# Attention of a two-layer decoder trunk: low parts of all weight panels on VectorE, and another order of scores, value sums and the late weight split

## The chip, the core and the metric

The kernel runs on one core of a Trainium2 chip. The metric is the device time of one execution in microseconds (us); lower is better. The core has a matrix engine (TensorE; PE in the profile, with its weight loads as PEld), three engines for elementwise work (VectorE or DVE, ScalarE or ACT, GpSimd or POOL) and queues that start transfers (those of SyncE, SP, and of GpSimd here). Each engine works through its own list of instructions in order, and the lists meet only at semaphores.

## The reference, cut to what matters

The input is one sequence of 512 tokens with 1024 features, in float32. Layer 0 has sixteen attention heads of 64 features: eight with a dilated window and a linear bias, eight with a forgetting bias. Layer 1 is a retention layer. Each is followed by a squared-ReLU MLP with 4096 hidden features, and a last norm closes the trunk. The change touches the attention of layer 0 alone.

```python
def _rms_norm(x, g):
    y = xf * lax.rsqrt(jnp.mean(xf * xf, axis=-1, keepdims=True) + RMS_EPS)
    return (y * g).astype(x.dtype)

def _dilated_branch(q, k, v, slopes, window, dilation):        # 8 heads
    logits = scores * dh**-0.5 - slopes * dist, masked to the dilated causal window
    # softmax inside each of the three dilations, then a softmax over their log-denominators

def _forgetting_attention(q, k, v, log_f):                     # 8 heads
    sc = q k^T * dh**-0.5 + c_i - c_j   (c = cumsum(log f)), causal
    return softmax(sc) @ v

def _even_mixer(h, w_in, b_f, w_out, slopes):
    proj = h @ w_in                    # q, k, v of both kinds of head, and the forget gates
    ...
    o = jnp.concatenate([_merge_heads(oa), _merge_heads(ob)], axis=-1)
    return o @ w_out

def reference(x, ...):
    for layer in range(2):
        h = _rms_norm(x, norm_mix_g[layer])
        x = x + (_even_mixer(h, ...) if layer % 2 == 0 else _odd_mixer(h, ...))
        h = _rms_norm(x, norm_ffn_g[layer])
        x = x + jnp.square(jax.nn.relu(h @ w1)) @ w2
    return _rms_norm(x, final_g)
```

## The kernel before

**Numbers in two parts.** Large products are not done in one float32 pass. An operand is kept as a high part (ScalarE rounds it with a copy) and a low part (the rest, by a subtraction), and three products are added: high by high, high by low, low by high. So each weight block of 128x128 costs three matmuls, and each weight panel has to be split before use: `split` on ScalarE (line 1460) writes the high part of a quarter of a panel, and a subtraction writes the low part. The subtraction is on VectorE (`split`, line 2107) for most panels, and on GpSimd (`split_lo`, line 3066) for panels 5 and 6 (`POOL_PANELS`).

**Panels and jobs.** Layer 0's projections use eight weight panels (`E_PANELS`: values, queries and keys by pairs of heads, and the two halves of the output weight). A panel has four quarters and serves four jobs; a job is eight k-tiles of three matmuls each with 512 columns, into one PSUM bank. Jobs 0 to 24 are the input projections (job 4 the gates, job 24, `LAST_KEY`, the last keys), jobs 25 to 32 the output projection, of which 25 to 28 use panel 6 and 29 to 32 panel 7.

**Attention beside the jobs.** `STEPS` and `TAIL` say which attention work stands beside which job. A step (h, g, v, pair) does four things: the scores of head h, the splitting of head g's probabilities into a high and a low f16 part, the value product of head v, and the transposition of a finished pair of heads. On PE, `beside` divides a step into ten points n = 0 to 9 that are spread between the k-tiles, and `attention` says what stands at which point: `gather_values(v)` (20 small matmuls, into `pv`), the three `scores_unit(h, u)` (u = 0 has 512 columns, u = 1 has 384, u = 2 has 256 and 128), and `turn_output(pair)`.

**What each head passes through.** PE scores; DVE `logits` (adds the bias table and takes the row maximum, line 2293); ACT `exps`; ACT `parts_hi` and DVE `parts_lo` (line 2302); the SP queue turns the parts by a DMA transposition into `turned_main`, one buffer for all heads but 13 and 15, which have their own; PE `gather_values`; DVE `value_sum` (a reduction, line 2314); GpSimd `normalise`; PE `turn_output`; ACT `output_hi` and DVE `output_lo` (line 2329) give the operand `oT` of the output projection. For heads 8 to 15 GpSimd adds the causal mask to the bias table just before each logits instruction (`mask`, line 3072), and the mask of the smallest query blocks waits until the logits of unit 1 are done.

**What sets the order.** Every engine's order is written out by hand. Scores use two banks in turn, so `scores_unit(h, 0)` waits for the first logits of head h - 1's unit 2. ACT copies a finished job to `q_stack` or `k_stack` (lines 1848 and 1852) only after that step's `exps`, and DVE takes the low part of it (lines 2388, 2392, and 2337 for job 24) before the next head's logits. The SP queue takes weight quarters and transpositions in one order; a quarter is fetched once `lo_split` says that the quarter before it in the same buffer is split. The k-tiles 6 and 7 of jobs 25 to 28 stand at the end (`EARLY_KT = 6`), after the last pair is transposed.

## Time and profile before

| | us |
|---|---|
| median of 3 runs (1263.57 to 1263.76) | 1263.6 |
| the profiled execution | 1263.39 |
| its span, first to last instruction | 1261.6 |
| PE busy (99% of the span) | 1243.1 |
| DVE busy (74%) | 932.4 |
| ACT busy (61%) | 767.5 |
| POOL busy (24%) | 296.6 |

The profiled execution lies 0.2 us from the median, and 1.8 us of it lie outside the span. Busy time is what an engine's instructions cover. A busy PE need not be at its best: its clock can be granted at half speed, and a matmul's duration holds its pipeline, so that the next one starts before it ends. The idle time of an engine that nobody waits for costs nothing.

### The profile page before, as it was taken

Reading aid. Unit: us, or ns where it says so; the run is one execution under the profiler, and the core shown is the slowest. Engines: PE = TensorE matmul, PEld = TensorE weight load, DVE = VectorE, ACT = ScalarE, POOL = GpSimd, SP = SyncE. Lnnn points to the kernel's source line nnn. Section 1 sums busy time; section 2 is a strip of 40 time slices with the busy share of each in tenths; the row PEclk is TensorE's granted clock in tenths of the full one; section 3 lists DMA queues with packets and bytes.
Section 4 is the critical chain, followed back from the end, with each engine's and each line's share of the span. In section 5 each row is a group of like instructions: output and inputs, shape, how many; then the busy total and the mean of one; then the engine's idle time right before and its main releaser. Section 6 shows DMA issues by size and latency. Waiting matters only on the chain.

```text
span 1261.6 us, 19374 instructions
## 1 busy us (share of the span) xinstructions
PE 1243.1 (99%) x7446; PEld 1096.2 (87%) x7446; DVE 932.4 (74%) x1196; ACT 767.5 (61%) x1064; POOL 296.6 (24%) x330
## 2 busy tenths in 40 slices
PE   9999998999999999999999999999999999999997
PEld 6788777798898988989898889898889899898996
DVE  6577646588759587598756797567899967859678
ACT  6677754477465474666646655556667757457474
POOL 2443653112111121111142212231231122111220
PEclk9999999999999999999999999999999999999999
DMA  7366456769998989983968597968589899898993
GB/s 249 91 142 153 120 150 130 242 139 229 229 236 209 226 170 235 233 234 93 214 132 184 155 244 165 225 145 221 110 220 242 199 212 228 215 235 198 207 217 101
DMA packets 147979, 238.95 MB, mean 189 GB/s; under 512 B 51104, under 2 KB 72872, under 8 KB 147888
## 3 DMA queue, kind: packets, MB, share of 16 engines
q0 software_dynamic: 32352, 102.79, 43.3%
q1 hardware_dynamic: 115232, 134.60, 34.0%
q8 instruction: 59, 0.97, 0.3%
q10 hardware_dynamic: 304, 0.33, 0.1%
q14 instruction: 32, 0.26, 0.1%
HBM read 127.57 MB, written 2.11 MB: 103 GB/s over the span
## 4 chain that ended last, share of the span: by engine, by line
PE 90%; DVE 4%; ACT 3%; issue 2%; DMA 1%; POOL 0%; SPq 0%; POOLq 0%; DVEq 0%; ACTq 0%
PE bank L945 22%; PE bank L977 18%; PE bank L1352 11%; PE bank L1420 6%; PE pv L977 5%; PE bank L1302 5%; PE bank L1143 4%; PE pv L945 4%; PE bank L1083 3%; PE bank L1244 2%; PE bank L1110 2%; PE bank L1316 1%; PE bank L1366 1%; PE pv L1366 1%; ACT arena L1781 1%
## 5 line engine op out<-in xcount | busy, mean ns | idle before, releaser
L2221 DVE TENSOR_TENSOR w<-raw_tiles,w 128x1024 fp32r<-128x1024 f32 x312 | 371.2, 1221 | 90.4 <-ACT w L1562 90.2
L1562 ACT ACTIVATE w<-raw_tiles 128x1024 fp32r<-128x1024 f32 x312 | 315.4, 1051 | 122.7 <-PE bank L977 56.2
L3159 POOL DMA_DIRECT2D raw_tiles<-raw_tiles x176 | 152.3, 908 | 629.5 <-DVE w L2221 360.0
L945 PE MATMUL bank<-h_ops,w 128*128 128x256 f32 x2304 | 281.4, 283 | 0.0
L945 PEld LDWEIGHTS bank<-h_ops,w 128*128 128x128 f32 x2304 | 278.9, 192 | 0.7
L977 PE MATMUL bank<-w,arena_q 128*128 128x512 f32 x1044 | 241.3, 389 | 0.0
L977 PEld LDWEIGHTS bank<-w,arena_q 128*128 128x128 f32 x1044 | 195.3, 188 | 40.1
L1352 PE MATMUL bank<-w,h_ops 128*128 128x512 f32 x624 | 143.9, 390 | 0.0
L1352 PEld LDWEIGHTS bank<-w,h_ops 128*128 128x128 f32 x624 | 116.6, 188 | 23.8
L1143 PE MATMUL bank<-hT_hi,w 128*128 128x512 f32 x224 | 78.2, 398 | 0.0
L1644 ACT ACTIVATE arena_q<-arena 128x1024 fp32r<-128x1024 f32 x40 | 42.5, 1062 | 47.0 <-PE pv L977 19.8
L1420 PE MATMUL bank<-w,arena_q 128*128 128x512 f32 x288 | 68.6, 393 | 0.0
L977 PE MATMUL pv<-w,arena_q 128*128 128x512 f32 x288 | 67.9, 389 | 0.0
L977 PEld LDWEIGHTS pv<-w,arena_q 128*128 128x128 f32 x288 | 54.1, 188 | 11.2
L1420 PEld LDWEIGHTS bank<-w,arena_q 128*128 128x128 f32 x288 | 53.3, 188 | 10.9 <-DVE x L2823 0.2
L2493 DVE TENSOR_TENSOR arena_q<-arena,arena_q 128x1024 fp32r<-128x1024 f32 x40 | 48.8, 1221 | 18.4 <-ACT arena_q L1644 17.8
L1302 PEld LDWEIGHTS bank<-h_ops,w 128*128 128x128 f32 x504 | 60.9, 192 | 0.2
L1302 PE MATMUL bank<-h_ops,w 128*128 128x256 f32 x504 | 60.9, 283 | 0.0
L1781 ACT ACTIVATE arena<-arena,negmax 128x512 f32<-128x512 f32 (+1 forms) x64 | 35.6, 558 | 34.2 <-DVE negmax L2293 34.2
L2471 DVE TENSOR_TENSOR arena<-arena,bank 128x512 f32<-128x512 f32 x48 | 32.7, 684 | 29.7 <-PE bank L945 29.7
L1143 PEld LDWEIGHTS bank<-hT_hi,w 128*128 128x128 f32 x224 | 42.1, 188 | 8.2
L945 PE MATMUL pv<-h_ops,w 128*128 128x256 f32 x384 | 48.7, 283 | 0.0
(268 smaller groups left out, 1817.8 us busy)
## 6 DMA issues: line engine op xcount, KB each, us to landing
raw_tiles<-raw_tiles POOLq DMA_DIRECT2D x176, 512.0 KB, 5.5
raw_tiles<-in_ffn_w_in SPq DMA_DIRECT2D x64, 512.0 KB, 5.8
raw_tiles<-in_ffn_w_out SPq DMA_DIRECT2D x64, 512.0 KB, 6.7
raw_tiles<-in_odd_w_in SPq DMA_DIRECT2D x32, 512.0 KB, 5.5
raw_tiles<-in_even_w_in SPq DMA_DIRECT2D x48, 256.0 KB, 3.3
raw_tiles<-in_odd_w_in SPq DMA_DIRECT2D x32, 256.0 KB, 5.3
raw_tiles<-in_odd_w_out SPq DMA_DIRECT2D x16, 512.0 KB, 6.0
raw_tiles<-raw_tiles POOLq DMA_DIRECT2D x20, 256.0 KB, 4.2
```

The lines of the kernel that those rows point to most:

```text
L945: mm = pe.matmul(bank[first + b][:, 256 * m:256 * m + 256], w_slots[use_slot(use)][:, p, k, c:c + P], h_ops[:, H_BLOCK[op], q, k, :], star ...
L977: mm = pe.matmul(bank[first + t][:, :], a_ring[a_slot(g, i)][:, a, k, P * t:P * t + P], w_slots[use_slot(use)][:, b, k, :], start=(starts ...
L1143: mm = pe.matmul(bank[e_bank(j)][:, :], stat(k, a), mov(k, b), start=(k == 0 and i == 0), stop=(k == KT - 1 and i == 2))
L1302: mm = pe.matmul(dst, w_slots[use_slot(use)][:, p, k, c:c + P], h_ops[:, H_BLOCK[op], q, k, :], start=(starts and k == 0 and n == 0), stop ...
L1352: mm = pe.matmul(bank[first + b][:, :], h_ops[:, H_BLOCK[op], p, k, P * b:P * b + P], w_slots[use_slot(use)][:, q, k, :], start=(i < 3 and ...
L1420: mm = pe.matmul(bank[first + t][:, :], operand[:, k, P * t:P * t + P], w_slots[use_slot(use)][:, b, k, :], start=(starts and m == 0), sto ...
L1562: nc.scalar.activation(w_flat(use_slot(use), 0, half), raws[tile][:, 1024 * half:1024 * half + 1024], ACT.Copy).then_inc(m_hi, 1)
L1644: nc.scalar.activation(a_ring[a_slot(g, i)][:, 0], a_source(1, op), ACT.Copy).then_inc(a_hi, 1)
L1781: nc.scalar.activation(v, v, ACT.Exp, bias=negmax[:, h % 2, c:c + 1], scale=-1.0, accum_out=den[:, pair % 2, k:k + 1]).then_inc(prob_ready, 1)
L2221: nc.vector.tensor_tensor(w_flat(use_slot(use), 1, half), raws[use_tile(key)][:, 1024 * half:1024 * half + 1024], w_flat(use_slot(use), 0, ...
L2493: nc.vector.tensor_tensor(slot[:, 1], a_source(1, SECOND[i][0]), slot[:, 0].bitcast(F32), ALU.subtract).then_inc(a_lo, 1)
L3159: pool.dma_start(raws[dst][:, part], raws[src][:, part], accum_op=ALU.add).then_inc(t_made[value][half], 16)
```

## The change

The change leaves the arithmetic alone. It moves eight subtractions from GpSimd to VectorE and writes several orders anew:

- The low parts of panels 5 and 6 (eight quarters) are taken by DVE: seven of them at the head of jobs 17 to 23, the eighth (quarter 3 of panel 6) after the first step of the tail. The high part of that eighth one moves on ACT from the end of job 24 to the same place of the tail.
- On PE the value product stands at point 2 in place of point 1 of the steps that have scores, except heads 12 and 15 (point 1) and 14 (point 0). The scores of heads 13, 14 and 15 move to later points.
- On DVE `value_sum` stands between the logits of units 1 and 2 (before: ahead of unit 1), and for heads 14 and 15 `value_sum` comes ahead of `parts_lo`, which is spread over the step.
- The k-tiles of jobs 25 to 28 stand in another order, with k-tile 6 of all four ahead of the last k-tile 7, which alone waits for the last pair.

```diff
@@ -331,7 +331,6 @@
 
 UNIT_BLOCKS = (4, 3, 3)
 UNIT_AT = (0, 8 * P, 14 * P)
-POOL_PANELS = range(5, 7)
 TURNS = ((0,), (1, 2))
 TURN_OF = {u: d for d, units in enumerate(TURNS) for u in units}
 
@@ -1182,9 +1181,9 @@
             def attention(h, g, v, pair, n):
 
 
-                if n == (0 if h == 14 else 1) and v is not None:
+                if n == {12: 1, 14: 0, 15: 1}.get(h, 2 if h is not None else 1) and v is not None:
                     gather_values(v)
-                at = (4, 6, 8) if h == 12 else (0, 3, 6)
+                at = {12: (4, 6, 8), 13: (1, 4, 7), 14: (4, 6, 8), 15: (2, 4, 6)}.get(h, (0, 3, 6))
                 if n in at and h is not None:
                     scores_unit(h, at.index(n))
                 if n == 5 and pair is not None:
@@ -1203,14 +1202,14 @@
                 beside(STEPS.get(j - 1, []), [(j, k) for k in range(KT)])
 
             last = STEPS[24]
-            beside(last[0:1], [(25, 0), (25, 1), (25, 2), (25, 3)])
-            beside(last[1:2], [(25, 4), (26, 0), (26, 1), (26, 2), (26, 3)])
-            beside(TAIL[0:1], [(26, 4), (25, 5), (26, 5), (27, 0), (27, 1), (27, 2)])
-            beside(TAIL[1:2], [(27, 3), (27, 4), (27, 5), (28, 0), (28, 1), (28, 2)])
-            beside(TAIL[2:3], [(28, 3), (28, 4)])
-            beside(TAIL[3:4], [(28, 5)])
+            beside(last[0:1], [(25, 0), (25, 1), (25, 2), (25, 3), (26, 0)])
+            beside(last[1:2], [(25, 4), (26, 1), (26, 2), (26, 3), (26, 4)])
+            beside(TAIL[0:1], [(27, 0), (27, 1), (27, 2), (25, 5), (26, 5)])
+            beside(TAIL[1:2], [(27, 3), (27, 4), (27, 5), (28, 0), (28, 1)])
+            beside(TAIL[2:3], [(28, 2), (28, 3), (28, 4)])
+            beside(TAIL[3:4], [(28, 5), (25, 6), (26, 6), (27, 6), (28, 6)])
             for j in range(25, 29):
-                out_part(j, range(EARLY_KT, KT))
+                out_part(j, [KT - 1])
             for j in range(29, 33):
                 e_job_free(j)
                 out_part(j, range(KT))
@@ -1855,8 +1854,6 @@
                         last.then_inc(aev, 1)
                     for st in STEPS.get(j, []):
                         step(*st, j + 1 if early_split(j + 1) else None)
-                    if j == LAST_KEY:
-                        split_for(j)
                 if n == 0:
 
                     act.wait_ge(job_done, GATE_JOB + 1)
@@ -1869,6 +1866,8 @@
                 if n == 5:
                     for st in TAIL:
                         step(*st)
+                        if st[1] == NHEAD - 1:
+                            split_for(LAST_KEY)
 
 
             norm_tiles(1)
@@ -2339,19 +2338,29 @@
                 done.then_inc(lev, 1)
 
             def step(h, g, v, pair):
-                if h is not None:
+                if h in (14, 15):
                     logits(h, 0)
-                if h == 14:
-                    dve.wait_ge(aev, e_aev(LAST_KEY))
-                    key_lo(LAST_KEY, 1)
-                if g is not None:
-                    for u in range(3):
-                        parts_lo(g, u)
-                if v is not None:
+                    if h == 14:
+                        dve.wait_ge(aev, e_aev(LAST_KEY))
+                        key_lo(LAST_KEY, 1)
                     value_sum(v)
-                if h is not None:
                     logits(h, 1)
+                    parts_lo(g, 0)
                     logits(h, 2)
+                    parts_lo(g, 1)
+                    parts_lo(g, 2)
+                else:
+                    if h is not None:
+                        logits(h, 0)
+                    if g is not None:
+                        for u in range(3):
+                            parts_lo(g, u)
+                    if h is not None:
+                        logits(h, 1)
+                    if v is not None:
+                        value_sum(v)
+                    if h is not None:
+                        logits(h, 2)
                 if pair is not None:
                     output_lo(pair)
 
@@ -2375,7 +2384,7 @@
                         for st in STEPS[j]:
                             step(*st)
                         continue
-                    if kind != "out" and n + 1 not in POOL_PANELS:
+                    if kind != "out" and j != LAST_KEY:
                         split(n + 1, q, n % 2)
                     if kind == "v":
                         value_rest_of(j)
@@ -2397,8 +2406,6 @@
                             dve.wait_ge(x_landed[q], 32)
                         residual(out_bank(j), i, q, j + 1)
                         if n < 7:
-                            if q == 0:
-                                dve.wait_ge(lo_split, 4 * 7)
                             split(n + 1, q, n % 2)
                         elif q < 2:
                             w_lo(0, 0, q)
@@ -2415,6 +2422,8 @@
                 if n == 5:
                     for st in TAIL:
                         step(*st)
+                        if st[1] == NHEAD - 1:
+                            split(6, 3, 1)
                 if n == 0:
 
                     dve.wait_ge(gate_low, 1)
@@ -3059,13 +3068,6 @@
                 nc.gpsimd.tensor_tensor(table[:, h % 2, :], table[:, h % 2, :], lncount,
                                         ALU.add).then_inc(table_ready, 1)
 
-            def split_lo(n, c):
-
-                pool.wait_ge(hi_split, 4 * n + c + 1)
-                pool.wait_ge(lo_split, 4 * n + c)
-                nc.gpsimd.tensor_tensor(panel_quarter((n + 1) % 2, 1, c), raw[:, c],
-                                        panel_quarter((n + 1) % 2, 0, c).bitcast(F32), ALU.subtract).then_inc(lo_split, 1)
-
             def mask(h, tb, dst=None):
 
                 own = table[:, h % 2, P * tb:P * tb + P]
@@ -3117,27 +3119,20 @@
             first_masks(9)
             bias_table(10)
             later_masks(9)
-            split_lo(5, 0)
             normalise(3)
             first_masks(10)
             bias_table(11)
             later_masks(10)
-            split_lo(5, 1)
             value_third(4)
             first_masks(11)
             bias_table(12)
             later_masks(11)
-            split_lo(5, 2)
             value_third(5)
             bias_table(13)
             first_masks(12)
-            split_lo(5, 3)
             value_third(6)
-            split_lo(6, 0)
             value_third(7)
-            split_lo(6, 1)
             later_masks(12)
-            split_lo(6, 2)
             first_masks(13)
             bias_table(14)
             normalise(4)
@@ -3148,7 +3143,6 @@
             normalise(5)
             first_masks(15)
             later_masks(15)
-            split_lo(6, 3)
             normalise(6)
             pool.wait_ge(score_done, 3 * NHEAD)
             load_gain(1)
```

Three places as the programs have them. First, VectorE beside job 24, in the step of head 13 (value product of head 10): `parts_f` is head 12's probabilities, `o_odd` the output of the value sum, and the rows with a bank are logits. Before:

```order
L2302 SCALAR_TENSOR_TENSOR parts_f<-arena,parts_f 128x512
L2302 SCALAR_TENSOR_TENSOR parts_f<-arena,parts_f 128x384 x2
L2314 TENSOR_REDUCE o_odd<-pv 128x4x64
L2319 RECIPROCAL rden<-den 128x8
L2293 ISA arena,negmax<-bank,arena 128x384
L2293 ISA negmax 128x1
L2293 ISA arena,negmax<-bank,arena 128x256
```

and now:

```order
L2301 SCALAR_TENSOR_TENSOR parts_f<-arena,parts_f 128x512
L2301 SCALAR_TENSOR_TENSOR parts_f<-arena,parts_f 128x384 x2
L2292 ISA arena,negmax<-bank,arena 128x384
L2292 ISA negmax 128x1
L2313 TENSOR_REDUCE o_odd<-pv 128x4x64
L2318 RECIPROCAL rden<-den 128x8
L2292 ISA arena,negmax<-bank,arena 128x256
```

The reduction and the reciprocal have moved behind the logits of 384 columns, ahead of those of 256 and 128.

Second, TensorE beside jobs 25 and 26, in the step of head 14, right behind the value product of head 11: rows with `arena_q` are scores, rows x3 with `arena_r` are k-tiles of the output projection. Before:

```order
L1040 MATMUL bank<-arena_q 128x512
L1042 MATMUL bank<-gain_q,arena_q 128x512
L1083 MATMUL bank<-w,arena_r 128x512 x3
L1040 MATMUL bank<-arena_q 128x384
L1042 MATMUL bank<-gain_q,arena_q 128x384
L1083 MATMUL bank<-w,arena_r 128x512 x3
L1040 MATMUL bank<-arena_q 128x256
L1042 MATMUL bank<-gain_q,arena_q 128x256
L1040 MATMUL bank<-arena_q 128x128
L1042 MATMUL bank<-gain_q,arena_q 128x128
L1083 MATMUL bank<-w,arena_r 128x512 x3
```

and now:

```order
L1082 MATMUL bank<-w,arena_r 128x512 x6
L1039 MATMUL bank<-arena_q 128x512
L1041 MATMUL bank<-gain_q,arena_q 128x512
L1082 MATMUL bank<-w,arena_r 128x512 x3
L1039 MATMUL bank<-arena_q 128x384
L1041 MATMUL bank<-gain_q,arena_q 128x384
L1082 MATMUL bank<-w,arena_r 128x512 x3
L1039 MATMUL bank<-arena_q 128x256
L1041 MATMUL bank<-gain_q,arena_q 128x256
L1039 MATMUL bank<-arena_q 128x128
L1041 MATMUL bank<-gain_q,arena_q 128x128
L1082 MATMUL bank<-w_raw,arena_r 128x512 x3
```

Two k-tiles now stand ahead of the first scores of head 14 (before: none), the third and the fourth, which opens job 26, stand ahead of the second and the third scores, and the k-tile of `w_raw` follows the scores.

Third, VectorE in the same step: `gain_q` is the low part of the last keys, a head at a time, and `parts_own_60` head 13's probabilities. Before:

```order
L2337 TENSOR_TENSOR gain_q<-bank,arena_q 64x512
L2293 ISA arena,negmax<-bank,arena 128x512
L2293 ISA negmax 128x1
L2337 TENSOR_TENSOR gain_q<-bank,arena_q 64x512
L2302 SCALAR_TENSOR_TENSOR parts_own_60<-arena,parts_own_60 128x512
L2302 SCALAR_TENSOR_TENSOR parts_own_60<-arena,parts_own_60 128x384 x2
L2314 TENSOR_REDUCE o_odd<-pv 128x4x64
L2293 ISA arena,negmax<-bank,arena 128x384
```

and now:

```order
L2336 TENSOR_TENSOR gain_q<-bank,arena_q 64x512
L2292 ISA arena,negmax<-bank,arena 128x512
L2292 ISA negmax 128x1
L2336 TENSOR_TENSOR gain_q<-bank,arena_q 64x512
L2313 TENSOR_REDUCE o_odd<-pv 128x4x64
L2292 ISA arena,negmax<-bank,arena 128x384
L2292 ISA negmax 128x1
L2301 SCALAR_TENSOR_TENSOR parts_own_60<-arena,parts_own_60 128x512
L2292 ISA arena,negmax<-bank,arena 128x256
```

The value sum and the logits of unit 1 have moved ahead of the splitting of head 13's probabilities, of which one part now stands between two logits.

## Rows read from the trace of the kernel before

**Rows 1.** PE's waits, 60 to 300 us: who for whom, us, times, longest.
```profile
PE bank L1040 <- DVE negmax L2293: 4.2, 3, 2.3
PE pv L1059 <- DMA turned_main<-parts_r: 1.8, 3, 1.0
PE bank L1040 <- DVE gain_q L2337: 1.4, 1, 1.4
PE bank L1083 <- DVE arena_r L2329: 0.7, 1, 0.7
PE bank L1070 <- DVE o_odd L2324: 0.4, 1, 0.4
PE pv L1059 <- issue: 0.4, 1, 0.4
```
**Rows 2.** Windows: length, each engine's busy time, granted clock, DMA share, GB/s.
```profile
201.00:206.00 5.00, 5.00 (x31) 4.38 (x30) 4.04 (x9) 2.57 (x10) 1.56 (x3) 0.66 0.41 77
255.00:600.00 345.00, 345.00 (x2271) 317.89 (x2270) 271.07 (x282) 216.40 (x250) 58.62 (x73) 1.00 0.83 203
```
**Rows 3.** PE in order of time: start, duration, instruction, idle before it.
```profile
65.34 0.39 PE L1143 MATMUL bank<-hT_lo,w_raw 128*128 128x512 f32 x1
...
66.03 0.39 PE L1143 MATMUL bank<-hT_lo,w_raw 128*128 128x512 f32 x1
...
72.23 0.26 PE L1059 MATMUL pv<-v_parts,turned_main 128*128 128x192 bf16 x1 [1.01 <-DMA turned_main<-parts_r]
...
193.97 0.47 PE L1040 MATMUL bank<-arena_q 128*128 128x512 f32 x1 [1.36 <-DVE gain_q L2337]
...
200.55 0.50 PE L1040 MATMUL bank<-arena_q 128*128 128x512 f32 x1 [2.30 <-DVE negmax L2293]
```
**Rows 4.** PEld in order of time, job 25 behind the scores of head 15.
```profile
209.04 0.53 PEld L1083 LDWEIGHTS bank<-w_raw,arena_r 128*128 128x128 f32 x3 [0.42 <-DVE arena_r L2329]
```
**Rows 5.** DVE in order of time, step of head 9.
```profile
137.56 0.94 DVE L2314 TENSOR_REDUCE o_odd<-pv 128x256 f32<-128x768 f32 x1
...
139.68 0.42 DVE L2293 CUSTOM_DVE_ANT_0 arena<-bank,arena 128x256 f32<-128x256 f32 x1 [0.71 <-POOL arena L3072]
```
**Rows 6.** POOL in order of time, at panel 6.
```profile
163.02 2.40 POOL L3066 TENSOR_TENSOR w<-raw_tiles,w 128x1024 fp32r<-128x1024 f32 x1
165.39 1.16 POOL L3045 TENSOR_TENSOR v_parts<-v_rest_f,v_parts 128x512 bf16<-128x512 f32 x1
```
**Rows 7.** DVE in order of time, at jobs 17 and 23.
```profile
141.79 0.69 DVE L2365 TENSOR_TENSOR v_rest_f<-bank,v_parts 128x512 f32<-128x512 f32 x1 [1.47 <-ACT v_parts L1838]
...
184.46 1.39 DVE L2388 SCALAR_TENSOR_TENSOR arena_q<-bank,arena_q 64x512 fp32r<-64x512 f32 x2 [2.06 <-ACT arena_q L1848]
```
**Rows 8.** Order of time around job 24: ACT.
```profile
191.93 2.40 ACT L1852 ACTIVATE arena_q<-bank 64x512 fp32r<-64x512 f32 x4
```
**Rows 9.** DVE in order of time, behind job 24.
```profile
193.14 0.68 DVE L2337 TENSOR_TENSOR gain_q<-bank,arena_q 64x512 fp32r<-64x512 f32 x1 [1.25 <-ACT arena_q L1852]
194.81 0.69 DVE L2293 CUSTOM_DVE_ANT_0 arena<-bank,arena 128x512 f32<-128x512 f32 x1 [0.98 <-PE bank L1042]
```
**Rows 10.** The buffer of the turned parts: time from issue to landing of its DMAs.
```profile
DMA to landing us min/median/max: 3.2/3.8/5.0
```
**Rows 11.** POOL and DVE in order of time, last quarter of panel 6.
```profile
210.22 2.38 POOL L3066 TENSOR_TENSOR w_raw<-raw_tiles,w_raw 128x1024 fp32r<-128x1024 f32 x1 [3.72 <-ACT w_raw L1460]
```
**Rows 12.** DVE in order of time, the same stretch, one instruction.
```profile
210.69 2.46 DVE L2302 SCALAR_TENSOR_TENSOR parts_own<-arena,parts_own 128x512 f16<-128x512 f32 x1 [1.71 <-ACT parts_own L1793]
```
**Rows 13.** DVE, 60 to 227 us: forms, count, busy us, mean ns, idle before.
```profile
L2107 DVE TENSOR_TENSOR w<-raw_tiles,w 128x1024 fp32r<-128x1024 f32 x6 | 7.5, 1254 | 0.0
L2302 DVE SCALAR_TENSOR_TENSOR parts_r<-arena,parts_r 128x512 f16<-128x512 f32 x10 | 6.9, 686 | 0.0
```
**Rows 14.** DVE in order of time, residuals of jobs 25 and 26.
```profile
227.35 0.69 DVE L2214 TENSOR_TENSOR x<-bank,x 128x512 f32<-128x512 f32 x1 [1.12 <-PE bank L1083]
...
229.09 0.69 DVE L2214 TENSOR_TENSOR x<-bank,x 128x512 f32<-128x512 f32 x1
```

## The prediction, made before the changed kernel had run

> **What bounds the kernel now.** I read the windows first, then PE's waits, then the order of time on each engine around every wait. From 255 to 600 us PE is busy in all 345.00 of 345 us at full clock [rows 2], and later stretches read the same: behind the attention the kernel is PE's own work, and whatever the attention saves or costs moves the end by as much. So the question is how much PE loses between 60 and 230 us. Its waits there are ten stops with 8.9 us together (4.2 + 1.8 + 1.4 + 0.7 + 0.4 + 0.4) [rows 1]. A stop costs more than its idle time: a matmul of 512 columns is drawn 0.39 us long, but three start within 0.69 us (65.34 to 66.03), one each 0.23 [rows 3], so idle time is counted from an end 0.16 us after the next start was due. Ten times 0.16 is 1.6. Behind the longest stop (2.30 us at 200.55, 1.36 us at 193.97 just ahead of it) [rows 3] the granted clock is 0.66 on average over 201 to 206 us [rows 2]: part of these 5 us ran at 1.2 in place of 2.4 GHz, and 5 x 0.34 = 1.7 us of work are lost. One wait is hidden in the weight loads, 0.42 us for the operand of pair 5 [rows 4]; PE covers some of it and I count 0.3. In all 8.9 + 1.6 + 1.7 + 0.3 = 12.5 us could be won, no more.
>
> **Value products a point later.** Three stops (1.8 us, the first 1.01) wait for the turned parts of a head [rows 1, 3]; the other two share 0.8. The transposition is released by `parts_lo`, whose place on DVE is the same, and the product now stands one k-tile, 0.69 us, later. Of the first stop 0.3 stays, the others go: 1.5, with two drains 1.8 us. Bounds: nothing (if the landing moves along) to 2.3.
>
> **The chain from logits to logits.** Two stops of 1.9 us together (4.2 less the 2.30) are first scores, of heads 10 and 13, that wait for the last logits of the head before [rows 1]. In the masked steps DVE does the value sum (0.94), then unit 1, and then idles 0.71 until GpSimd has masked for unit 2 [rows 5]; eight such waits exist. With the value sum between the two that idle time is covered: each masked step is 0.7 shorter on DVE, and ACT's exponentials of unit 1 run beside the value sum. Ahead of head 10 two such steps follow each other, 1.4 against a stop of 0.99; head 13 gets 0.7 and a k-tile of 0.69 more on PE against 0.9. Both go: 1.9 with two drains 2.2. Bounds: 0.7 (the shorter chain alone, once) and 2.2.
>
> **Eight subtractions from GpSimd to DVE.** GpSimd needs 2.40 for one, and `value_third` starts only behind it: 163.02 + 2.40, then 1.16 to 166.5 [rows 6], where the value product of head 8 stops for 0.4 with "issue" as releaser [rows 1]. That stop goes: 0.6 with its drain. On DVE a split takes 1.25 [rows 13]. At jobs 17 to 23 DVE idles seven times ahead of the row that the split now precedes, least at the first (1.47) and 2.06 at the last [rows 7]; the eighth place, in the tail, has more than 2 us too. The cover is ACT's copy of a finished job or GpSimd's third value part, and each idle time is longer than the split, so I take zero; without cover each costs 1.25, all eight 10.
>
> **Heads 14 and 15.** The copy of the last keys runs on ACT from 191.93 [rows 8], behind head 13's exponentials; its low part is done at 193.14 + 0.68 = 193.8 [rows 9], and head 14's first scores start at 193.97 after 1.36 idle [rows 3]. Two masked steps (12 and 13) now end 0.7 earlier each, so these scores may start near 192.5. PE arrives, by its own work, at 193.97 - 1.36 = 192.6, less 1.06 for the stop of head 13, plus 2 x 0.69 for the two k-tiles put ahead: 192.9. No stop is left. Call that start s. DVE's answer begins 0.84 later (194.81 against 193.97) [rows 3, 9]; logits and the second low part of the keys end at s + 2.25, value sum at 3.1, unit 1 at 3.65, the first third of `parts_lo` (0.69) [rows 13] at 4.35, unit 2 at 4.8. PE asks for that at the first scores of head 15: scores, three k-tiles, a value product of 1.4 and a last k-tile put them at s + 6.2. So the 2.30 goes too, and with it the reason of the low clock: 1.36 + 2.30 + 1.7 + two drains = 5.7, and the hidden 0.3. Bounds: 0.7 to 6.0. New is a wait inside: k-tile 0 of job 26 needs the bank of job 24, hence the second low part of the keys at s + 2.25, and PE is there after scores, k-tile and scores (0.46 + 0.69 + 0.35) at s + 1.5: **0.8 us lost**, 0 to 1.5. Behind that stop nothing but PE queues; DVE does not wait for it. Also new: value products 10, 11 and 12 stand closer together (heads 13, 14 and 15 use three different points), and each transposition into the one buffer starts when the product before has read it. A landing takes 3.8 us, 5.0 at most [rows 10]; against some 5.5 us between products the margin is used up by the issue of two DMAs. I take **0.5** of 0 to 2.4.
>
> **The tail.** Two stops, 0.4 and 0.7 [rows 1], wait for the last pair. Now k-tiles 6 of jobs 25 and 26 stand ahead of its transposition (1.4 us against 0.4 + 0.16) and two k-tiles behind it, 1.4, where one k-tile and the stop made 0.69 + 0.16 + 0.72 = 1.6: **0.2 stays**. Won: 1.4 in all. But jobs 25 to 28 now end 0.69 apart, not 1.38, and behind each DVE adds the residual and splits a quarter of panel 7: 1.74 us a pair (227.35 to 229.09) [rows 14]. The fourth quarter is ready some 0.2 + 4 x 1.74 = 7.2 us after job 25; PE asks for it at 3 x 0.69 + 3 x 1.38 = 6.2. **1.1 lost** with a drain, 0 to 1.5; before, it was asked for at 8.3 and cost nothing.
>
> **Sum.** Won: 1.8 + 2.2 + 0.6 + 5.7 + 0.3 + 1.4 = 12.0. New or left inside: 0.8 + 0.5 + 0.2 + 1.1 = 2.6. From the profiled execution, 1263.4: 1263.4 - 9.4 = **1254.0**. That execution lies 0.2 under the median, so the median reads the same within it.
>
> **A rule against the change.** A split reads two operands in SBUF while GpSimd masks read theirs. The trace shows such a pair once: GpSimd's subtraction runs from 210.22 to 212.60 [rows 11], and DVE's first third of `parts_own`, started at 210.69, takes 2.46 in place of 0.69 [rows 12, 13], that is until 0.55 after GpSimd's end. The Trainium skill (SBUF — State Buffer, "SBUF: two separate sides") calls the port that these two engines share an exclusive lock that is held for the whole instruction; by that rule the trace agrees. It cuts both ways: the 1.8 us at 210 go with GpSimd's subtractions (DVE has them to spare there), and each new DVE split can hold a mask up for 1.25.
>
> **Rivals.** (1) The late order stays bound by another engine: heads 14 and 15 still wait for DVE, ACT or the mask, at other places, and the clock still falls. For it: DVE has five kinds of work within 6 us there; against it: the slack of 1.4 found above. 5.7 of the win is gone, part of the new waits too: 1263.4 - 4.2 = 1259.2. (2) The landings follow the products, since one buffer serves them: 1.8 is not won and 0.3 more is lost at heads 11 and 12: 1256.1. For it: one buffer; against it: the stops came with an early release by the product and a late one by `parts_lo`. (3) Splits block masks: three of the eight stand just ahead of a masked head (jobs 17, 18, 23), 1.25 each on the logits' chain: 1257.8. Against it: at jobs 17 to 22 PE has whole jobs without scores to catch up. (4) The other side: DVE becomes the bound. If the idle times at jobs 17 to 23 are used up, because ACT and PE arrive earlier as well, the eight splits lie on the chain to PE, 8 x 1.25 = 10.0, and two waits long enough to bring the clock down add 2 x 1.7: 1254.0 + 13.4 = 1267.4. It decides once the splits cost over 9.4, that is nearly all of them; the shortest idle time, 1.47, is over a split. (5) The new orders never meet the waits: same time as before, 1263.4.
>
> **Chances.** Forecast 0.62, rival 1 0.15, rival 2 0.11, rival 3 0.06, rival 4 0.03, rival 5 0.03. The range: best case 1263.4 - 12.5 = 1250.9 needs every bound at its good end; I start at 1251.5, and take in rivals 1, 2 and 3 up to 1260.0. A measurement here tells 0.2%, 2.5 us, from no change. Faster than 1261.1: 0.92; within: 0.05; slower: 0.03.
>
> **What would show it.** Right: PE's waits between 60 and 230 us sum to 2 to 3.5 us; none over 1.2; the granted clock is 1.00 in every window there; no 0.71 of DVE for a mask in steps with a value sum; DVE's splits at jobs 17 to 23 with hardly a change of PE; short waits for `w` at k-tiles 2, 4 and 6 of job 29. Wrong: a stop over 1.5 us near the last keys, a second one at each value product, or a window at half clock.

## The result, and the profile after

The changed kernel takes 1254.41 us (median of 4 runs, 1254.35 to 1255.75) against 1263.61 for the kernel before (1263.57 to 1263.76): a ratio of 0.993 with an interval of [0.9912, 0.9947]. The forecast was 1254.0. The profiled execution took 1254.46 with a span of 1252.3, 9.3 less than the span before. Line numbers of PE, DVE and ACT in the kernel after are one smaller than before: L1058 and L1060 are the value product, L1039 and L1041 the scores, L1082 the k-tiles, L2292 the logits, L2313 the value sum, L2106 a split.

PE's waits of the kernel after, 60 to 300 us (waiting line and releaser: us in total, times, longest), answer to [rows 1]:

```profile
PE pv L1058 <- DMA turned_main<-parts_r: 1.3, 2, 0.8
PE bank L1082 <- DVE gain_q L2336: 0.6, 1, 0.6
```

Ten stops with 8.9 us have become three with 1.9 (2 to 3.5 were forecast). The windows of the kernel after (busy time of PE, PEld, DVE, ACT, POOL with instructions, then the granted clock, DMA share and GB/s) answer to [rows 2]:

```profile
60.00:230.00 170.00, 167.93 (x999) 138.80 (x998) 126.28 (x263) 117.04 (x255) 61.22 (x65) 1.00 0.64 156
201.00:206.00 5.00, 5.00 (x40) 4.21 (x38) 4.61 (x8) 2.65 (x6) 1.37 (x1) 1.00 0.90 169
255.00:600.00 345.00, 344.98 (x2238) 316.40 (x2237) 271.93 (x286) 213.78 (x248) 60.77 (x73) 1.00 0.84 205
```

The same stretch of the kernel before, in the same view:

```profile
60.00:230.00 170.00, 161.01 (x957) 132.16 (x956) 110.97 (x248) 112.64 (x251) 74.89 (x72) 0.99 0.60 143
```

PE is busy 6.9 us more in the 170, and the clock no longer falls. DVE has 15 us more to do there and GpSimd 14 less: the subtractions moved, and the stretch now reaches some 9 us further into the program. Behind 255 us PE is as busy as it was, so the lead is carried to the end undiminished: the same instruction (the first transposition of the second norm) starts at 242.08 before and 232.69 after, 9.4 earlier.

What is left sits in three places. First PE, by the order of time; one row for each stop:

```profile
72.19 0.26 PE L1058 MATMUL pv<-v_parts,turned_main 128*128 128x192 bf16 x1 [0.55 <-DMA turned_main<-parts_r]
...
187.31 0.26 PE L1058 MATMUL pv<-v_parts,turned_main 128*128 128x192 bf16 x1 [0.77 <-DMA turned_main<-parts_r]
...
191.84 0.96 PE L1082 MATMUL bank<-w,arena_r 128*128 128x512 f32 x3 [0.58 <-DVE gain_q L2336]
```

The first is the stop of head 2, once 1.01 and now a k-tile later; the second is new, in the value product of head 11: the transposition that it waits for is issued at 180.58, right behind the last matmul of head 10's product (180.28), which now stands a k-tile later; the third is k-tile 0 of job 26 behind the second low part of the keys. Then weight loads (PEld of the kernel after, with the idle time ahead of each row), which answer to [rows 4]. The first row is the last k-tile of jobs 25 to 28, which waits for the operand of the last pair; the others belong to job 29:

```profile
217.59 2.61 PEld L1082 LDWEIGHTS bank<-w_raw,arena_r 128*128 128x128 f32 x12 [0.45 <-DVE arena_r L2328]
220.60 1.22 PEld L1082 LDWEIGHTS bank<-w,arena_r 128*128 128x128 f32 x6 [0.40 <-issue]
222.27 1.23 PEld L1082 LDWEIGHTS bank<-w,arena_r 128*128 128x128 f32 x6 [0.45 <-DVE w L2106]
224.00 1.23 PEld L1082 LDWEIGHTS bank<-w,arena_r 128*128 128x128 f32 x6 [0.51 <-DVE w L2106]
```

A third wait for `w`, of 0.51 too, follows at 225.73. The three fall every 1.73 us, which is DVE's pace (the kernel after, DVE):

```profile
220.40 0.68 DVE L2213 TENSOR_TENSOR x<-bank,x 128x512 f32<-128x512 f32 x1
221.00 1.21 DVE L2106 TENSOR_TENSOR w<-raw_tiles,w 128x1024 fp32r<-128x1024 f32 x1
222.13 0.68 DVE L2213 TENSOR_TENSOR x<-bank,x 128x512 f32<-128x512 f32 x1
222.73 1.21 DVE L2106 TENSOR_TENSOR w<-raw_tiles,w 128x1024 fp32r<-128x1024 f32 x1
```

Residual and split take DVE 1.73 a pair, as in [rows 14], and PE's two k-tiles take 1.38: job 29 walks behind DVE. Last, a masked step of DVE in the kernel after (head 12), against [rows 5]:

```profile
175.57 0.54 DVE L2292 CUSTOM_DVE_ANT_0 arena<-bank,arena 128x384 f32<-128x384 f32 x1
176.05 0.07 DVE L2292 DVE_READ_ACCUMULATOR2_ANT negmax<- 128x1 f32 x1
176.05 0.94 DVE L2313 TENSOR_REDUCE arena<-pv 128x256 f32<-128x768 f32 x1
176.92 0.41 DVE L2292 CUSTOM_DVE_ANT_0 arena<-bank,arena 128x256 f32<-128x256 f32 x1
```

The value sum stands between unit 1 and unit 2, and no idle time stands ahead of unit 2: the 0.71 is gone.

### The profile page after: what moved, and what is told of

It reads as the page before. It is cut to its first block, busy times and chain, and to the rows that moved or that the text cites. A ratio compares the mean times of both kernels' runs of the same rounds, so it can differ in the third digit from the quotient of the medians.

```text
span 1252.3 us, 19365 instructions
## 1 busy us (share of the span) xinstructions
PE 1240.8 (99%) x7446; PEld 1095.0 (87%) x7446; DVE 940.9 (75%) x1204; ACT 768.4 (61%) x1064; POOL 282.5 (23%) x322
## 4 chain that ended last, share of the span: by engine, by line
PE 95%; DVE 2%; DMA 1%; issue 1%; ACT 1%; SPq 0%; POOLq 0%; POOL 0%; DVEq 0%; ACTq 0%
PE bank L944 22%; PE bank L976 18%; PE bank L1351 11%; PE bank L1142 7%; PE bank L1419 6%; PE pv L976 5%; PE bank L1301 5%; PE pv L944 4%; PE bank L1082 3%; PE bank L1243 2%; PE bank L1109 2%; PE bank L1315 1%; PE bank L1365 1%; PE pv L1365 1%; PE pv L1058 1%; PE pv L1351 1%
```

## The experiments

All times are compared with runs of the kernel before on the same chip. Three groups of runs gave medians of 1263.42, 1263.67 and 1262.67 for it. These differ since its executions fall into two groups, around 1262.0 and around 1263.6; under `fill_stops` stands what the runs show of the reason. The intervals belong to the ratios. Differences under 1 us between medians of such mixed executions say little.

**splits_only**: the kernel before with the eight subtractions on DVE.

```diff
-                    if kind != "out" and n + 1 not in POOL_PANELS:
+                    if kind != "out" and j != LAST_KEY:
                         split(n + 1, q, n % 2)
...
-            split_lo(5, 0)
...
```

> The kernel before with the eight subtractions of panels 5 and 6 on VectorE, every order else as before. Theory of the prediction (each split stands in idle time of VectorE): the stop of 0.4 us before head 8's value product goes, about 0.6 us faster, 1263.0; the clock still falls near 202 us. Rival (VectorE is the bound, the splits lie on its chain): up to 8 x 1.25 = 10 us slower, and the first scores of heads 10 to 14 wait longer for logits. Rival (the shared port: splits hold up masks): 1 to 4 us slower.

1262.96 us, ratio 0.9994 [0.9984, 1.0003]. The stop of head 8's value product with releaser "issue" is gone, and no other has grown by as much (a new one of 0.27 stands at head 11's product): PE's stops sum to 8.3. So the 10 us of new DVE work are free, as forecast, and what they win is too small for the ratio to tell from nothing. Taken group by group, which the interval does not cover, it may be the forecast 0.6: the three lowest of the ten runs lie at 1261.4 to 1261.6, the five lowest of the 20 of the kernel before at 1261.9 to 1262.3.

**value_sum_only**: the kernel before with the value sum between units 1 and 2, except at heads 14 and 15.

```diff
-                if v is not None:
+                if h in (14, 15):
                     value_sum(v)
-                if h is not None:
                     logits(h, 1)
                     logits(h, 2)
+                else:
+                    if h is not None:
+                        logits(h, 1)
+                    if v is not None:
+                        value_sum(v)
+                    if h is not None:
+                        logits(h, 2)
```

> The kernel before with one move on VectorE: the value sum stands between the logits of units 1 and 2 for all heads but 14 and 15. Theory: each masked step is 0.7 us shorter on VectorE, so the stops before the first scores of heads 10 and 13 (0.99 and 0.90 us) go, and head 14's first scores (1.36) wait some 1.4 less: 2.2 to 4.5 us faster, 1259.1 to 1261.4. Rival (the chain is bound by ACT's copies of finished jobs, not by VectorE): under 1 us.

1258.08 us, ratio 0.9963 [0.9949, 0.9977]. PE's waits of this kernel:

```profile
PE bank L1040 <- DVE negmax L2293: 2.3, 1, 2.3
PE pv L1059 <- DMA turned_main<-parts_r: 1.0, 1, 1.0
PE bank L1083 <- DVE arena_r L2329: 0.7, 1, 0.7
PE bank L1070 <- DVE o_odd L2324: 0.4, 1, 0.4
PE bank L1040 <- DVE gain_q L2337: 0.3, 1, 0.3
```

This is the largest single part, 4.7 by the ratio (the interval allows 2.9 to 6.4), more than the theory had even at its best (1259.1). The spans of two profiled executions in both of which the clock fell, 1261.6 and 1257.1, lie 4.5 apart. It reaches further than its own stops. Those ahead of the first scores of heads 10 and 13 are gone, but also two of the three for turned parts and the one of 0.4 in head 8's value product, and head 14's stop has shrunk from 1.36 to 0.29. The 2.3 of head 15 stays.

**gather_only**: the kernel before with the value products a point later, nothing else.

```diff
-                if n == (0 if h == 14 else 1) and v is not None:
+                if n == {12: 1, 14: 0, 15: 1}.get(h, 2 if h is not None else 1) and v is not None:
                     gather_values(v)
```

> The kernel before with one move on TensorE: the value product one point later for the heads that the change moves. Additive theory (as in the prediction's sum): the waits for turned parts at heads 2, 5 and 8 shrink by 0.69, 0.37 and 0.44 us, 1.8 us faster with drains, 1261.8. Rival (the chain of VectorE and ACT sets when head 10's first scores may start, whatever TensorE gained before): the stop of 0.99 us there grows by what was won, and the time stays 1263.6.

1262.44 us, ratio 0.9997 [0.9988, 1.0007]. PE's waits of this kernel:

```profile
PE bank L1040 <- DVE negmax L2293: 4.8, 4, 2.3
PE bank L1040 <- DVE gain_q L2337: 1.1, 1, 1.1
PE bank L1083 <- DVE arena_r L2329: 0.7, 1, 0.7
PE pv L1059 <- DMA turned_main<-parts_r: 0.6, 1, 0.6
```

The waits for turned parts fell from 1.8 to 0.6, and those for logits rose from 4.2 to 4.8, with one new stop of 0.30 ahead of head 8's first scores and head 10's grown from 0.99 to 1.29. About half of what was removed came back: PE arrives earlier at scores whose bank DVE frees at the same time as before. With the two stops not shown (0.4 each) the sum is 8.0 against 8.9. The median lies between the two forecasts; the ratio allows 1.5 us at most, less than the 1.8 of the additive theory. The five lowest of the ten runs (1261.5 to 1261.8) again lie some 0.6 under the five lowest of the kernel before.

**late_undone**: the changed kernel with the old orders of heads 13 to 15 and of jobs 25 to 28.

```diff
-                at = {12: (4, 6, 8), 13: (1, 4, 7), 14: (4, 6, 8), 15: (2, 4, 6)}.get(h, (0, 3, 6))
+                at = (4, 6, 8) if h == 12 else (0, 3, 6)
...
-            beside(TAIL[3:4], [(28, 5), (25, 6), (26, 6), (27, 6), (28, 6)])
+            beside(TAIL[3:4], [(28, 5)])
...
```

> The changed kernel with the orders of heads 13, 14 and 15 and of the k-tiles of jobs 25 to 28 put back (TensorE and VectorE), all else as changed. Theory: the early wins stay (1.8 + 2.2 + 0.6 = 4.6 us), the late ones (5.7 + 0.3 + 1.4 less 2.6 new) go: 1259 to 1260, with a stop of over 2 us before head 15's first scores and half clock behind it. Rival (the shorter chain on VectorE removes the late stops by itself, the new late order adds little): 1255 to 1256.5.

1257.18 us, ratio 0.9952 [0.9938, 0.9967]. Head 15's stop of 2.29 is back, with the low clock behind it, and the two tail stops. The general part is thus worth 6.1 by the ratio, and the late orders the rest of the change's 8.8, some 2.7, where I had split the sum about evenly. The time lies between both forecasts.

**late_only**: the counterpart, the kernel before with the late orders alone.

```diff
-                if n == (0 if h == 14 else 1) and v is not None:
+                if n == {13: 2, 14: 0}.get(h, 1) and v is not None:
...
-                at = (4, 6, 8) if h == 12 else (0, 3, 6)
+                at = {12: (4, 6, 8), 13: (1, 4, 7), 14: (4, 6, 8), 15: (2, 4, 6)}.get(h, (0, 3, 6))
...
+            beside(TAIL[3:4], [(28, 5), (25, 6), (26, 6), (27, 6), (28, 6)])
...
```

> The kernel before with the late orders alone: scores, value products and DVE's order of heads 13 to 15, and k-tiles of jobs 25 to 28; the value sum stays ahead of unit 1 in all other heads, and the subtractions stay on GpSimd. Theory: the late orders work by themselves, since k-tiles ahead of the first scores of heads 14 and 15 fill both stops whenever these scores come: 1263.6 less 1.36, 2.30, 1.7 and 1.0, plus 1 to 2 for new waits: 1258.3 to 1259.5. Rival (additive): they are worth what taking them out of the changed kernel cost, 2.6 to 2.8: 1260.8 to 1261.2. Second rival: without the shorter chain DVE and ACT stay late at heads 13 to 15 and a stop of over 1.5 us comes back: 1262 to 1264.

1260.64 us, ratio 0.9983 [0.9974, 0.9992]. PE's waits of this kernel:

```profile
PE pv L1059 <- DMA turned_main<-parts_r: 2.4, 5, 1.0
PE pv L1059 <- DVE arena L2314: 1.7, 1, 1.7
PE bank L1040 <- DVE negmax L2293: 1.2, 2, 1.0
PE bank L1083 <- DVE gain_q L2337: 0.6, 1, 0.6
PE pv L1059 <- issue: 0.4, 1, 0.4
```

Both stops of heads 14 and 15 are gone without the shorter chain, and the clock stays at 1.00 in every window from 190 to 230 us. In their place one value product stops for 1.71 until DVE has read the sum before it. The first theory missed. The additive rival, 1260.8 to 1261.2, was nearest: worth 2.1 alone and some 2.7 on top of the rest, which the intervals do not tell apart.

**splits_back**: the changed kernel with the subtractions back on GpSimd.

```diff
-                    if kind != "out" and j != LAST_KEY:
+                    if kind != "out" and n + 1 not in POOL_PANELS:
                         split(n + 1, q, n % 2)
...
+            split_lo(5, 0)
...
```

> The changed kernel with the eight low-part subtractions of panels 6 and 7 back on GpSimd, all orders as changed. Theory (the move paid for the value product of head 8 and little else): 1254.5 + 0.6 = 1255.1, and up to 1256.5 if GpSimd's last subtraction, 2.4 us long, holds DVE's low parts of head 15 up at 210 us as in the kernel before (2.46 in place of 0.69), now with no slack on PE. Rival: the shorter chain has no slack for GpSimd's 2.4 us at jobs 17 to 23, masks come late, and three or more stops of 1 us or over come back: 1258 or more. Second rival: the move is worth nothing any more, since the product stands a k-tile later: 1254.3 to 1254.8.

1254.6 us, ratio 0.9934 [0.992, 0.9947], and the same three stops as the changed kernel (0.75, 0.43 and 0.59). The second rival held: once the product stands a k-tile later, the move of the subtractions brings nothing to the total, and costs nothing. The spans show two small parts in it. The median span is 1252.8 here and 1252.4 in `changed_again`, so the move wins some 0.4 inside the span. But between 1.7 and 1.9 us lie outside the span in every run of a kernel whose subtractions are on GpSimd, and 2.1 to 2.2 in every run of one that has them on DVE. Why is not shown.

**changed_again, swap_26, tail_spaced**: the changed kernel again, and two repairs, one for the wait inside job 26 and one for the pace of the tail.

```diff
-            beside(last[0:1], [(25, 0), (25, 1), (25, 2), (25, 3), (26, 0)])
-            beside(last[1:2], [(25, 4), (26, 1), (26, 2), (26, 3), (26, 4)])
+            beside(last[0:1], [(25, 0), (25, 1), (25, 2), (25, 3), (25, 4)])
+            beside(last[1:2], [(26, 0), (26, 1), (26, 2), (26, 3), (26, 4)])
```

```diff
-            beside(TAIL[3:4], [(28, 5), (25, 6), (26, 6), (27, 6), (28, 6)])
-            for j in range(25, 29):
-                out_part(j, [KT - 1])
+            beside(TAIL[3:4], [(28, 5)])
+            for j, k in ((25, 6), (26, 6), (27, 6), (25, 7), (26, 7), (27, 7), (28, 6), (28, 7)):
+                out_part(j, [k])
```

> The changed kernel once more, on the chip of the three that follow, as their base: 1254.4 us, or 9.2 below the kernel before.

> The changed kernel with two k-tiles exchanged: job 25's fifth stands where job 26's first stood, ahead of the last scores of head 14, and job 26's first comes one scores unit later. Theory (the stop of 0.58 us there is the wait for the second low part of the last keys, with 0.16 of drain): it goes, and head 12's value product comes as early as before: 0.7 us faster, 1253.7. Rival (the chain of VectorE to head 15's scores is the bound behind it): the 0.7 comes back as a stop before head 15's first scores, time the same.

> The changed kernel with the last pair's transposition two k-tiles earlier and jobs 25 to 28 ending further apart: 25.6 26.6 27.6 25.7 26.7 27.7 28.6 28.7 behind the transposition. Theory (VectorE's 1.74 us a job for residual and split is late for job 29, three waits for w of about 0.5 us, and one of 0.45 for the last operand): these go but for 0.3: 1.3 to 1.7 us faster, 1252.7 to 1253.1. Rival (the weights of the MLP behind it, or the norm, then are the bound): under 0.3 us.

1254.54 (0.9931 [0.9918, 0.9943]), 1253.98 (0.9927 [0.9913, 0.994]) and 1253.68 (0.9926 [0.9913, 0.9938]). The intervals against the kernel before overlap, and so do the ranges of the runs (1254.27 to 1254.87, 1253.60 to 1254.53, 1253.60 to 1254.69). The differences thus rest on the medians of five runs each, 0.56 (0.7 was expected) and 0.86 (1.3 to 1.7), and on what is missing from the profiles: the 0.58 for `gain_q` in the one, and the last operand's wait with one of the three for `w` in the other. From PEld's waits of tail_spaced, 180 to 240 us, the two of line 1082:

```profile
PEld bank L1082 <- DVE w L2106: 0.9, 2, 0.5
PEld bank L1082 <- DVE gain_q L2336: 0.9, 1, 0.9
```

The repair of the tail brought less than expected, since DVE still paces job 29 in part: two waits for `w` are left.

**all_mended, best**: both repairs, and the value products in the steps of heads 2 and 14 at points 3 and 2 (heads' scores and k-tiles around them unchanged); then `best` with head 15's product at point 3, behind its first scores, too, and on DVE another order of residuals and quarters of panel 7: the residual of job 26 behind two quarters, that of job 27 behind all four.

```diff
-                if n == {12: 1, 14: 0, 15: 1}.get(h, 2 if h is not None else 1) and v is not None:
+                if n == {12: 1, 14: 2, 2: 3, 15: 3}.get(h, 2 if h is not None else 1) and v is not None:
...
-                            split(n + 1, q, n % 2)
+                            if q == 0:
+                                residual(out_bank(j), i, 0, j + 1)
+                                split(7, 0, 0)
+                                split(7, 1, 0)
...
```

> The changed kernel with both edits, and the value products of the steps of heads 2 and 14 later (points 3 and 2 in place of 2 and 0), where 0.55 and 0.77 us are waited for turned parts. Theory (all stops left are of those four kinds): 0.7 + 1.5 + 0.7 + 0.9 = 3.8 us faster, 1250.6. Rival (a later value product in the step of head 14 delays the transposition for head 12, which then lands late): 1251.5, with a stop before head 12's value product.

> The changed kernel with what the runs so far point to: job 25's k-tile 4 ahead of job 26's first, jobs 25 to 28 closing further apart, value products of heads 14, 2 and 15 at points 2, 3 and 3, and on DVE the residual of each job ahead of split quarters for which PE has no need yet. Theory: no stop of PE over 0.3 us is left between 60 and 230 us, 0.5 less than the last version of 1252.62 for the stop at head 15 and 0.9 to 1.4 less for weight waits of job 29: 1250.7 to 1251.3. Rival: PE has no waits worth the name left there, and the rest is spread over weight loads and issue; 1252.0 to 1252.8.

1252.62 (1251.95 to 1253.69), 0.9916 [0.9902, 0.993], and 1252.13 (1251.84 to 1252.43), 0.9912 [0.9899, 0.9926]. For `all_mended` both forecasts missed, the theory's 1250.6 by 2 us: the parts of 0.7, 1.5, 0.7 and 0.9 did not add up. In `all_mended` one stop of 0.51 is left; `best` has one too, a longer one (the row is PE's, in order of time):

```profile
193.53 0.50 PE L1039 MATMUL bank<-arena_q 128*128 128x512 f32 x1 [1.13 <-DVE negmax L2292]
```

Head 15's product, put behind its first scores, let PE reach these 1.13 too early. That part of the theory for `best` was wrong. What DVE's order in the tail won (there is no wait left on PEld behind 214 us) made up for it, and no more can be said: the ranges of the two kernels overlap. Both beat the changed kernel by about 2 us. The theory's time, 1250.7 to 1251.3, missed by a us, and the rival's, 1252.0 to 1252.8, holds the measured one, though its picture of no stop worth the name does not.

**fill_stops**: the kernel before, with matmuls nobody reads in the two long stops.

```diff
+                for _ in range({14: 10, 15: 19}.get(h, 0) if u == 0 else 0):
+                    pe.matmul(bank[4][:, 0:256], ident[:, 0:64].bitcast(BF16), ident[:, :].bitcast(BF16), start=True, stop=True)
```

> The kernel before, with matmuls that compute nothing used put on PE ahead of the first scores of head 14 (10 of 256 columns, about 1.1 us) and of head 15 (19, about 2.0 us), where PE otherwise stops for 1.36 and 2.30 us. Nothing else is changed. Theory: the low granted clock behind the 2.30 us stop is PE's answer to the idle time, and it costs about 1.7 us of work where it falls; filled, the clock stays at 1.00 over 190 to 206 us and the kernel takes 1261.7 to 1262.1 (1263.6 less 1.7, plus 0 to 0.3 for fillers that end late). Rival: the clock costs nothing on the path there, since the scores and logits that follow wait for other engines anyway; then 1263.4 to 1264.0.

1262.45 us (1262.0 to 1263.43), ratio 0.9997 [0.9988, 1.0005]: the median lies in neither forecast, nearer to the first (1261.7 to 1262.1) than to the second (from 1263.4). Its clock is 1.00 from 190 to 230 us, and one of its eleven runs is above 1263.3 where nine of 21 of the kernel before are. That one had a late start (below).

Two other observations bear on the same question. The stop of head 15 is as long in splits_only as in value_sum_only, 2.29 and 2.28, but the windows behind it differ. First splits_only, whose profiled execution took 1261.64, among the three lowest of its ten:

```profile
196.00:201.00 5.00, 2.71 (x18) 1.83 (x17) 3.49 (x11) 1.74 (x7) 2.13 (x4) 1.00 0.93 174
201.00:206.00 5.00, 5.00 (x39) 4.46 (x37) 4.25 (x12) 3.12 (x8) 1.46 (x3) 1.00 0.56 106
```

Then value_sum_only:

```profile
196.00:201.00 5.00, 4.91 (x28) 4.17 (x29) 3.80 (x11) 3.04 (x9) 2.10 (x4) 0.66 0.24 45
```

After one and the same stop the clock stays in some executions and falls to 1.2 GHz in others (in the kernel before it reads 0.50 in each microsecond from 202 to 205); where it falls, 5 x 0.34 = 1.7 us go. The ten runs of splits_only lie at 1261.4 to 1261.6 (three) and 1262.7 to 1263.8 (seven), those of the kernel before at two values as far apart. And the mean clock that each run of the kernel before reports goes with its group: of the 50 runs beside the experiments, all 19 under 1263 read 0.999, and 24 of the 31 over it read 0.997 or 0.998. The reading is coarse (some runs of kernels with the clock at 1.00 in every window read 0.998 too), and the seven others may be late starts. So the clock is the likely cause of the upper group; the filled kernel agrees with that without proving it.

## Why the prediction was right, and which of its steps were not

**What bounds the kernel**: right. All gain was made ahead of 232 us and carried to the end; 9.4 forecast, 9.2 measured between the medians, 8.9 between the profiled executions. Their spans differ by 9.3: idle 8.9 to 1.9, seven drains less (1.1) and the clock 1.7 make 9.8, and the 0.5 left over fits the weight waits that were not there before (it is the remainder, not a measurement). Of the 9.3, 0.4 are lost outside the span, a part that the sum did not have (`splits_back`). With `changed_again`, five more runs agree (1254.54).

That the total came so near is in part luck. Several terms below are off by a factor of two or more and make up for each other, and the 1.7 of the clock stands in the sum as certain: all four runs of the kernel before in the first comparison were of the upper group. Against the lower group, around 1262.0, the same changed kernel is some 7.6 faster.

**Value products** (1.8 forecast): right in what stops remained (0.55 at the first, against 0.3 forecast), wrong in the cause. Alone the move won less than that, nothing by the ratio and perhaps 0.6 (gather_only), for PE met the logits' chain instead, and value_sum_only removed two of the three stops without it. So these two landings were late with the chain. My bound "nothing, if the landing moves along" named another reason: the landing did not move, and the next wait took the gain.

**The chain** (2.2): the mechanism was right, the size wrong by a factor of two. It measured 4.7 (2.9 to 6.4). I counted the idle time of the two heads at which PE stopped, but the shorter step is earned at many heads, and it is spent wherever PE waits for anything that hangs on DVE's step: products, logits, the last keys. It is not earned at masked heads alone. One of the products that stopped, at 106.23, is that of head 4 (in the step of head 6; the expectation of gather_only has it at head 5), ahead of all masked heads. In head 5's step the logits of unit 1 no longer stand behind the value sum, and ACT's exponentials of unit 1 start after 0.25 us of idle time in place of 1.11; from head 4's first logits to head 5's DVE takes 9.18 in place of 9.64 (value_sum_only against before). The prediction counted masked steps only. The terms of the sum were not independent, so the products' 1.8, head 8's 0.6 and head 14's 1.5 were booked under other edits. Each stop was counted once, which is why a total can hold while its parts do not.

**Subtractions** (0.6): cost zero as forecast, but beside the rest of the change the win was zero too (splits_back). GpSimd's masks take longer. Both forms, after and then before:

```profile
L3074 POOL TENSOR_TENSOR arena<-arena,causal 128x128 f32<-128x128 f32 x24 | 16.2, 680 | 37.7 <-DVE negmax L2292 37.5
L3074 POOL TENSOR_TENSOR first_block<-arena,causal 128x128 f32<-128x128 f32 x8 | 5.9, 738 | 2.0 <-DVE negmax L2292 2.0
```

```profile
L3072 POOL TENSOR_TENSOR arena<-arena,causal 128x128 f32<-128x128 f32 x24 | 14.5, 609 | 37.6 <-DVE negmax L2293 37.6
L3072 POOL TENSOR_TENSOR first_block<-arena,causal 128x128 f32<-128x128 f32 x8 | 3.7, 458 | 1.1 <-DVE negmax L2293 1.1
```

The second form is the dearer one, 0.28 us a mask, and most of that comes with the moved splits: it takes 695 ns in splits_only, 458 in value_sum_only and 503 in splits_back. DVE's splits lengthen as well, to 1335 ns from 1254 [rows 13], but not by the move: their mean is 1253 in splits_only and 1350 in value_sum_only, where the eight subtractions are on GpSimd. The new place of the value sum does it, because GpSimd's `normalise`, which the sum releases, now runs into a split: the split at 85.67 takes 1.81 us in place of 1.22, with `normalise` at work from 85.35 to 86.39. So the two engines do hold each other up, yet rival 3 did not come: no stop of PE follows from it.

**Heads 14 and 15** (5.7 and 0.3, less 0.8 and 0.5): both stops and the low clock went. DVE at the turn in the kernel after, against [rows 9]:

```profile
190.36 0.69 DVE L2292 CUSTOM_DVE_ANT_0 arena<-bank,arena 128x512 f32<-128x512 f32 x1 [2.26 <-PE bank L1041]
...
191.09 0.69 DVE L2336 TENSOR_TENSOR gain_q<-bank,arena_q 64x512 fp32r<-64x512 f32 x1
191.81 0.96 DVE L2313 TENSOR_REDUCE o_odd<-pv 128x256 f32<-128x768 f32 x1
192.80 0.56 DVE L2292 CUSTOM_DVE_ANT_0 arena<-bank,arena 128x384 f32<-128x384 f32 x1
```

DVE now waits 2.26 for PE's scores, where PE had waited for DVE. The place of the meeting was off: I had head 14's first scores at 192.9 and they start at 189.60, since I took only head 13's stop off PE's arrival, though most of the earlier ones go as well. From there on the working fits: the second low part is done 2.2 behind these scores (2.25 forecast), and head 15's first scores come 6.3 behind them (6.2). The inner wait measured 0.58 against 0.8, the stop at a late landing 0.77 against 0.5. Rival 1 (DVE stays the bound here) is what value_sum_only looks like: the shorter chain alone leaves 2.3. Together these orders brought some 2.7 (late_undone) with the tail's, where my terms for both had 4.8, since a part of theirs was the chain's. The clock term was right for an execution in which the clock falls; it does not fall in every one.

**The tail** (1.4 won, 0.2 and 1.1 left): both stops went, and the last operand left 0.45 and `w` three waits of about 0.5 on PEld. tail_spaced puts the price of this at 0.9 or more, by medians whose ranges overlap (1.1 and 0.2 forecast).

## What to carry to other kernels

When several engines chase each other through one chain, a stop on the bound engine belongs to the chain and not to the edit that names its releaser: count each stop once for the total, but expect the edit that shortens the chain to earn most of it and the one that only moves the waiter to earn little alone. Before an instruction is moved later past a wait, look what the engine meets next and how much slack that has. An order that closes several jobs in a row must leave each reader of them (here DVE's 1.73 us a quarter) its own pace.

## What the runs showed of the hardware

Two things were not expected. The first is the clock above: a stop of 2.3 us is followed by 1.2 GHz in some executions (value_sum_only) and not in others (splits_only). The second is at the start. PE begins with matmuls at half the rate and reaches the full one at different times. Three equal matmuls in the kernel before:

```profile
6.90 0.81 PE L1006 MATMUL bank<-arena 128*128 128x512 bf16 x3
```

The same three in the profiled execution of all_mended:

```profile
8.36 1.49 PE L1005 MATMUL bank<-arena 128*128 128x512 bf16 x3
```

ACT's first copy of a product (`hT_hi`) then starts at 10.70 in place of 8.81, and that execution took 1253.69, where the lowest of the same kernel took 1251.95. The profiled executions of gather_only (10.75) and fill_stops (10.30) show the same. In gather_only's the clock fell too (0.67 from 200 to 205 us), and it took 1265.08 where the lowest run took 1261.47: 3.6 more, as much as the 1.7 of the clock and the 1.9 of the start together. The granted clock is given as 1.00 in these microseconds in all of them, so the column does not show this half rate; the durations do. With differences of 0.5 us between kernels, five runs are few against two such switches.
